# Cache pages loaded as 64 rows of 4 KB instead of 128 rows of 2 KB, in a hybrid attention and mLSTM decoder step

## The reference, cut to what matters

```python
def _moba_sample(q, k, v, cache_k, cache_v, page_table):        # q (8, 8, 8 heads, 64)
    ...
    kb_past = cache_k[page_table[:, :nb_full * ppb]].reshape(DB, nb_full, MOBA_BLOCK, H, D)
    k_mean = jnp.mean(kb_past, axis=2, dtype=jnp.float32)
    idx, valid = _moba_select(q, k_mean, nb_full)              # the 3 best of 8 blocks, by q . k_mean
    logical = idx[..., None] * ppb + jnp.arange(ppb)
    phys = page_table[jnp.arange(DB)[:, None, None, None, None], logical]
    k_sel = cache_k[phys, :, h_i].reshape(DB, H, T, K, MOBA_BLOCK, D)
    v_sel = cache_v[phys, :, h_i].reshape(DB, H, T, K, MOBA_BLOCK, D)
    ...                                                        # softmax over the 3 blocks and the own tokens
```

## Time and profile before

| what | us |
|---|---|
| median of 3 runs (1118.14 to 1120.73) | 1119.84 |
| the profiled execution, its own time | 1118.83 |
| its span in the profile | 1117.2 |
| TensorE busy, share of the span | 1066.3 (95%) |
| TensorE weight loads busy | 910.2 (81%) |
| VectorE busy | 563.8 (50%) |
| ScalarE busy | 449.5 (40%) |
| GpSimd busy | 126.6 (11%) |
| decoding sequences' attention, first keys to last values | 347.6 to 600 |

### The profile page before, as it was taken

How to read it: one execution, slowest core, us unless ns; L and a number is a source line. 1 busy time by engine, 2 the same in 40 slices (tenths; PEclk the granted TensorE clock), 3 DMA queues, 4 the chain that set the end, 5 groups by cost and what they waited for, 6 DMA issues and landing times.

```text
span 1117.2 us, 20695 instructions
## 1 busy us (share of the span) xinstructions
PE 1066.3 (95%) x7593; PEld 910.2 (81%) x7593; DVE 563.8 (50%) x1227; ACT 449.5 (40%) x1023; POOL 126.6 (11%) x227
## 2 busy tenths in 40 slices
PE   4999999999999999999988998999999999999997
PEld 4977877887777777767768886998899899889985
DVE  5254534545675655655644747443344334433456
ACT  5253233324554555555543355342144113322441
POOL 4003110221001033323331100100000000000000
PEclk8999999999999999999999999999999999999999
DMA  6432216234136799989974440223222222222222
GB/s 214 117 86 57 67 48 142 57 85 124 48 96 188 202 326 309 322 308 339 321 218 132 150 134 29 95 76 94 84 77 86 85 76 86 80 81 85 77 85 85
DMA packets 93716, 150.02 MB, mean 134 GB/s; under 512 B 9377, under 2 KB 39590, under 8 KB 93622
## 3 DMA queue, kind: packets, MB, share of 16 engines
q1 hardware_dynamic: 75040, 103.83, 30.6%
q0 software_dynamic: 11968, 39.85, 10.6%
q10 hardware_dynamic: 6614, 5.06, 1.6%
HBM read 141.62 MB, written 7.10 MB: 133 GB/s over the span
## 4 chain that ended last, share of the span: by engine, by line
PE 78%; DVE 9%; issue 4%; ACT 3%; DMA 3%; SPq 1%; POOLq 1%; ACTq 1%; POOL 0%; DVEq 0%
PE ps L462 27%; PE ps L497 19%; PE ps L890 7%; PE ps L470 4%; PE ps L1919 4%; PE ps L906 3%; PE ps L435 2%; DMA kring<-in_cache_k_dram 2%; PE ps L1928 1%; PE ps L1960 1%; DVE xn L552 1%; PE ps L1054 1%; PE ps L1074 1%; PE ps L1064 1%; ACT sP L2036 1%
## 5 line engine op out<-in xcount | busy, mean ns | idle before, releaser
L347 DVE TENSOR_TENSOR w<-w,w 128x512 fp32r<-128x512 f32 (+1 forms) x240 | 168.0, 706 | 305.6 <-ACT w L336 301.0
L336 ACT ACTIVATE w<-w 128x512 fp32r<-128x512 f32 (+1 forms) x240 | 145.2, 613 | 337.7 <-PE ps L470 172.4
L497 PE MATMUL ps<-h2T,w 128*128 128x288 f32 x1536 | 210.0, 297 | 4.3 <-DVE wide L2529 1.7
L497 PEld LDWEIGHTS ps<-h2T,w 128*128 128x128 f32 x1536 | 207.1, 189 | 7.2 <-DVE wide L2529 2.4
L462 PE MATMUL ps<-w,hid 128*128 128x512 f32 x672 | 161.6, 389 | 0.0
L462 PEld LDWEIGHTS ps<-w,hid 128*128 128x128 f32 x672 | 125.9, 188 | 26.0
L462 PE MATMUL ps<-w,hT 128*128 128x512 f32 x576 | 145.3, 401 | 1.4 <-ACT ri L811 1.4
L462 PEld LDWEIGHTS ps<-w,hT 128*128 128x128 f32 x576 | 106.0, 190 | 26.6 <-issue 4.9
L890 PE MATMUL ps<-hT,w 128*128 128x288 f32 x768 | 124.2, 305 | 0.0
L890 PEld LDWEIGHTS ps<-hT,w 128*128 128x128 f32 x768 | 104.7, 188 | 11.3 <-issue 10.6
L1886 POOL DMA_DIRECT2D vring<-in_cache_v_dram x128 | 68.8, 538 | 180.1 <-issue 180.1
(11 more groups left out here) (354 smaller groups left out, 1279.1 us busy)
## 6 DMA issues: line engine op xcount, KB each, us to landing
kring<-in_cache_k_dram SPq DMA_DIRECT2D x128, 256.0 KB, 4.1
vring<-in_cache_v_dram POOLq DMA_DIRECT2D x128, 256.0 KB, 4.5
w<-in_w_in_dram SPq DMA_DIRECT2D x88, 256.0 KB, 2.9
w<-in_w_up_dram SPq DMA_DIRECT2D x64, 256.0 KB, 2.8
w<-in_w_down_dram SPq DMA_DIRECT2D x64, 256.0 KB, 2.8
w<-in_w_out_dram SPq DMA_DIRECT2D x16, 256.0 KB, 3.0
x<-in_x_prompt_dram SPq DMA_DIRECT2D x4, 512.0 KB, 6.9
out_dram<-sC ACTq DMA_DIRECT2D x1, 2048.0 KB
```

The source lines that it names most:

```text
L336: eng.activation(spread(w_hi, n, j, width), together(w32, n, j, width), ACT.Copy)\
L347: eng.tensor_tensor(spread(w_lo, n, j, width), together(w32, n, j, width), spread(w_hi, n, j, width).bitcast(F32), ALU.subtract).then_inc( ...
L497: mm = eng.matmul(ps[:, b, 0:HALFT], w[a][:, j, i * P:(i + 1) * P], right[c][:, k, h * HALFT:(h + 1) * HALFT], start=(k == 0 and (c, a) == ...
```

## The change

In `pages`, which issues the loads of keys and of values alike, a page is read as 64 rows of two tokens (4 KB) in place of 128 rows of one token (2 KB). The ring is seen as 4 pairs of slots. Page j of a group goes into pair j // 2; a row of it lies across both slots of the pair on one partition. The first page of a block (j even) takes the even partitions, the second (j odd) the odd ones, so the two pages of a block fill the pair of slots together. Tokens 2p and 2p+1 of page j are now on partition 2p + j % 2, one in the first slot of the pair and one in the second. Keys and values get the same layout, and nothing that reads the rings is changed.

```diff
     def pages(eng, pool, ring, arrived, b, g):
 
-        flat = pool.rearrange("n p h d -> n p (h d)")
+        flat = pool.rearrange("n (p two) h d -> n p (two h d)", two=2)
+        two = ring[:, :, :].rearrange("p (a two) c -> p a (two c)", two=2)
         for j in range(4):
             page = eng.value_load(pt_sb[0:1, bass.ds(b * NPAGE + g * 4 + j, 1)],
                                   min_val=0, max_val=pool.shape[0] - 1)
-            eng.dma_start(ring[:, 4 * (g % 2) + j, :], flat[bass.ds(page, 1), :, :].rearrange("a p n -> (a p) n"))\
+            eng.dma_start(two[j % 2:P:2, 2 * (g % 2) + j // 2, :],
+                          flat[bass.ds(page, 1), :, :].rearrange("a p n -> (a p) n"))\
                .then_inc(sem(f"{arrived}{g % 2}"), 16)
```

## The result

The changed kernel takes 1124.49 us in the median of 20 runs (1120.20 to 1131.74), the kernel before 1119.51 us (1114.37 to 1126.84). The ratio is 1.005, with a 95% interval of 1.0033 to 1.0066. It is slower, by 5 us where 1140 us had been forecast, some 20 more: the sign came out, the size did not. The profiled execution took 1122.38 us, with a span of 1120.7.

What follows compares the result with a forecast made beforehand. TensorE's work and the DMA transfers were taken to stand level in the decoding sequences; 1118.8 us profiled, +19 for sequences 3 to 8 and +0.6 for the tail gave 1138.5, as a median about 1140 us, range 1114 to 1185.

Steps and rivals of the forecast that it cites:

- the sign: Whole kernel: direction of the change, slower given 0.50, same 0.17, faster 0.33.
- the sum of excesses: Decoding sequences: waits for keys beyond 0.84 us, 0.81, 0.11, 1.27 and 2.12, put at 4.3 us in all.
- the cover: Before a wait for keys: 0.84 us in which TensorE still runs score matmuls, so only the excess is lost.
- The packet: Page loads: engines meet half the time, a 4 KB packet takes 208 ns, a page 0.83 us; chance 0.38.
- The bound of 297 ns: Page loads: upper bound for a 4 KB packet, from the y_sample store's 64 neighbouring partitions; a page 1.19 us.
- The +19 us of the sum: Sequences 3 to 8: DMA busy time rises from 157.3 to 181.3 us, needing 189 at share 0.96: +19.
- The issue on SyncE: Issue of keys: +0.2 us a page, 0.8 a group, counted as 0 while the engines' backlog covers it.
- The faster rival: Page loads: engines do not meet, a packet takes 160 ns, waits for keys go, about 1116 us; chance 0.33.
- A packet above 185 ns: Sequences 3 to 8: 5.9 us of room allows packets up to 185 ns; above that the kernel gets slower.
- The last sentence of the prediction: If the stage lengthens while packets stay below 185 ns, the forecast is wrong and the cause is issue, not transfer.
- The tail: After the last key loads: GpSimd issue unchanged (0), last page's landing grows 0.15 us in about four groups: +0.6.

Runs made afterwards that it cites:

- its second profile: The changed kernel executed and profiled once more, nothing altered; median 1125.53 us, ratio 1.0064 to the kernel before.
- keys alone: Against the kernel before, only keys loaded as 64 rows of 4 KB on every second partition, values keeping 128 rows of 2 KB; 1122.77 us, ratio 1.0017.
- the second pair: Both kernels executed and profiled once more, unaltered; medians 1125.53 us for the changed kernel and 1122.04 us for the kernel before.
- the early numbers: A key group's four page numbers read ahead of the k_free wait on SyncE; changed kernel 1115.49 us (0.9950), kernel before 1114.94 us (0.9945).
- early numbers on that queue: Kernel before, rows of 2 KB, with page numbers read ahead of the waits on both SyncE and GpSimd; 1111.71 us, ratio 0.9932.
- two runs a row: Changed kernel with each of the 64 rows made of two runs of 2 KB, tokens p and p + 64; 1131.07 us, ratio 1.0112.

## Why the prediction was wrong

**What bounds the kernel.** Right: TensorE's order and the transfers stood level, and the waits for kring were what could move. Two waits of the kernel before had been left out (1.52 us at 541 us and 0.91 at 562, 0.75 above the cover), so the sum of excesses was 5.1 and not 4.3.

**The packet: the step that failed.** "The mean rate is (1/160 + 1/297) / 2, a packet takes 208 ns, a page 0.83 us. I take this value". By the same kind of window, 180 ns were measured for keys and 174 for values in the changed kernel (202 and 171 in its second profile, 163 and 166 with keys alone). Over the whole stage a packet of keys cost 5 to 9 ns more than before and one of values 6 to 12 less, where the forecast had added 25 and 37. The idea was that engines get neighbouring blocks of rows and meet at the same group of partitions. Packets are that slow when the 64 rows lie on neighbouring partitions (276 ns). On every second partition most are not: half take 159 ns or less, and every tenth of the keys' 296 or more. Whether those are engines that meet is open. The bound of 297 ns was real for rows on neighbouring partitions, and the new layout is not half way to it. The +19 us of the sum was all built on this step, and none of it is there: both queues' shares of the span are what they were.

**The issue on SyncE: the mis-sized term.** The rows were read rightly (+0.2 us a page by estimate, +0.137 measured), and then the term was set to nothing: "While the engines are the bound, their backlog covers it: 0". Since the packets of both queues together did not get dearer, no backlog was there to cover it, and behind k_free the fourth page has hardly any slack. An addition of 0.44 us a group, with old packets, costs 5.1 us by its ratio; the change's 0.44 to 0.58 us a group costs 5 to 7. The faster rival had this term too, and had it too small: "0.8 us in the two or three groups that wait today". In fact further groups came to wait, 11 above 0.84 us in place of 6.

**The rivals.** The faster one had the packet nearer (160 forecast, 163 to 202 measured for the keys in windows of pages alone, 200 and 204 over the stage) and the conclusion wrong, because transfers that stay as cheap do not shorten anything that the issue decides. "A packet above 185 ns makes the kernel slower; this is the point that decides between the signs" is refuted: the two queues cost the engines what they had cost, and the kernel is slower. That the sign came out is luck, since the forecast drew it from dearer packets. The last sentence of the prediction named this case, a longer stage with packets that do not get dear, and its cause.

**The tail.** "0 in issue" for GpSimd was right (537 and 536 ns). That the tail would lengthen by 0.6 was wrong. It got 3.0 us shorter, as a pause of 3.4 us of GpSimd left it (2.8 in the second pair). In both profiles of the kernel before, TensorE waits 3.6 us for values right behind that pause (the row at 583.27 of the earlier trace rows), and its granted clock then falls to about half for some us; in the changed kernel that wait is 1.6 us and the clock stays at 1.00. The merge then got 2.6 us longer (1.5 in the second pair): x is issued 3.3 us after the sum that it waits for, where it had been 0.3, and TensorE waits 2.4 us (1.3) on VectorE before the matmuls of `wo_res`. That the one causes the other is likely and wasn't followed.

**What stays open.** The ratio's interval is worth 3.7 to 7.4 us, while the two pairs of profiles show 0.4 to 2.9 us in the sequences and 2.7 to 2.9 us in the excess. Adding the issue's time to the old layout makes a loss of the same size, and taking the page numbers off the path removes the loss. That shows that the issue is enough; it doesn't show that all of the loss is issue. The slack of the early numbers would also hide a landing that is a little later, and the run with keys alone is 1.9 us slower, not 5. What makes GpSimd pause is open too.

## What to carry to other kernels

Where a ring is refilled behind a semaphore, count everything that the issuing queue does between that semaphore and the last DMA of the refill, and move what doesn't depend on it ahead of the wait. Here reading four page numbers earlier is worth 5 us, while larger rows are worth nothing and cost 5. And before the cost of an edit is set to nothing because a backlog covers it, ask what is left if the backlog isn't there.

## What the runs showed of the hardware that was not expected

- On SyncE a DMA of 64 rows took longer to issue than one of 128 rows: 475 ns against 338 for a page; with two runs a row 605. On GpSimd the same three took 536, 537 and 619 ns. The weight loads that stand right behind the pages on SyncE went from 433 to 590 ns (median of the eight of `w_mlstm_br`).
- GpSimd's queue already joined two rows of 2 KB into packets of 4 KB (11968 packets before and after); SyncE's made one packet for each run.
- 64 rows of 4 KB on every second partition took 183 to 204 ns a packet in the mean of the stage (half of them 159 or less), about what 128 rows of 2 KB took for 4 KB (192 to 195), and 276 on neighbouring ones.
- Behind waits for kring of 3.2 to 3.6 us the granted clock of TensorE went to 0.50 for about 3 us in three profiles; behind waits of 3.2 and 3.3 us in two others it stayed at 1.00.
- Pages of values of 128 runs went with a GpSimd pause at the second page of the fourth group from the end, 3.4 us in seven profiles and 2.8 in the one with early numbers on that queue. In the six profiles with values in rows of 4 KB it was missing there, and x was issued 3.3 us after its sum in place of 0.3.
